# Expert loop of a two-layer trunk: down weights requested from ScalarE's queue instead of SyncE's

## The chip, the cores and the metric

The kernel runs on one core of one Trainium2 chip. The metric is the device time of one execution in microseconds. The engines are named as the profile names them: PE (TensorE), DVE (VectorE), ACT (ScalarE), POOL (GpSimd) and SP (SyncE). SP computes nothing here; it waits on semaphores and issues DMAs.

## What is computed

Two layers of a transformer trunk over 384 tokens of 1024 features (128 context tokens, 256 latent ones). Each layer has a mixing part (four attention-like branches) and then a mixture of experts. Only the latter is touched. Cut to what matters:

```python
scores = jax.nn.sigmoid((t @ lp['w_router']).astype(jnp.float32))
...
w = w / jnp.sum(w, axis=-1, keepdims=True) * ROUTE_SCALE
combine = jnp.sum(jax.nn.one_hot(eidx, N_EXPERTS, dtype=jnp.float32) * w[..., None], axis=1)
gu = jnp.einsum('nd,edf->nef', t, lp['w_exp_gu'])
a = jax.nn.silu(gu[..., :EXPERT_FF]) * gu[..., EXPERT_FF:]
a = (a * combine[..., None].astype(a.dtype)).reshape(-1, N_EXPERTS * EXPERT_FF)
routed = a @ lp['w_exp_down'].reshape(N_EXPERTS * EXPERT_FF, D_MODEL)
```

There are 32 experts a layer; every token goes to 4 of them. An expert has a gate-up matrix of 1024 x 512 (2 MB in fp32) and a down matrix of 256 x 1024 (1 MB).

## The kernel before

The tokens' choices are sorted into tiles of at most 96 rows, one expert a tile; an expert with more rows gets further tiles at the end. The loop over tiles goes two tiles a turn (`e` is 0 or 1, the tile's slot); the number of turns is read from a table, and here it is 16, so there are 32 tiles a layer and 64 in all.

For one tile the work is this. GpSimd gathers the tile's rows from DRAM into `xg` (`gather`, L1139). PE turns them (`turn_gathered`, L2337), ScalarE and VectorE split them into a rounded part and the rest (`x_high` L1454, `x_low` L1976). All products are made of three matmuls over such parts, so the weights are split as well: ScalarE rounds each landed gate-up half (`gu_high`, L1449) and VectorE writes the rest over it (`gu_low`, L1970); the same for the down weights (`dn_high`, L1461, two copies; `dn_low`, L1984). PE's `gate_up` (L2349) has 24 matmuls in two halves of 12, `down_split` (through L2051) 12. ScalarE takes the silu (L1492), VectorE the product (`product`, L1902), PE turns it (`turn_product`, L2293), ScalarE rounds that (L1485). The results of the down product stand in two banks of PSUM; ScalarE copies them to `yrow` (L1497, two copies a tile), and GpSimd scatters them to DRAM (`scatter`, L1150).

The order on each engine is written out in its own `steps(turn)`. PE's step for a tile is: turn the rows gathered for a later tile, turn the tile's product, gate-up of the next tile, down product of this tile. ScalarE's step is: round the gathered rows, round the turned product, round both gate-up halves for the tile after next, silu of the next tile, round the next tile's down weights, copy this tile's results. `W` holds two slots for gate-up weights (each two halves) and two for down weights.

All weights are asked for by SP (L943 for gate-up halves, L946 for down weights), one queue in the order of issue. Its step for a tile: once PE is through the first gate-up half of the next tile (`gu_half`), load that half for the tile after; once it is through the second, load the second; once this tile's down product has filled its second bank (`y1`), load the down weights of the tile after next into this tile's slot. The expert's number is read from a table in SBUF (`expert_u`, L973) ahead of each address. After the loop, in layer 0, SP loads the first four pieces of the next layer's weights (`load_front`, L993 and L997).

Of the kernel before, what the change touches and what calls it, by code (L numbers as in the profile page):

```python
# [19 lines left out]
P = 128  # L20
# [19 lines left out]
NE, TOPK, NG, TOPG, FF = 32, 4, 4, 2, 256  # L40
# [297 lines left out]
def trunk(nc, a):  # L338

    with ExitStack() as ctx:  # L340
# [3 lines left out]
        def sb_twice(name, n):  # L344
# [51 lines left out]
                 "gqa_ready", "kdup_ready", "diff_roped", "qm_roped", "km_ready", "max_ready",  # L396
                 "pd_ready", "lam_ready", "absx_ready", "expx_ready", "u_ready", "ln_ready", "lg_ready",
                 "dec_ready", "qkfb_ready", "masks_raw", "mask_ready", "state_ready", "state_out", "ro_ready",
                 "do_ready", "gate_ready", "merged_ready", "m_squared", "x_ready", "chosen_ready", "slots_ready", "ones_ready", "gathers", "sp_steps", "table_reset", "slots_out", "table_in", "rows_out", "tables_ready", "summed", "silu_ready",
                 "lam_dots", "lam_exps", "head_normed", "mean_ready", "ret_squared", "branch_rs"]  # L400
        names += ["bias_in0", "bias_in1", "bias_zero", "mod_gain", "gates_out", "gates_in", "cache_out"] + [f"{n}{i}" for n in ("x_landed", "y_written", "index_copied", "place_copied") for i in range(2)]
        names += [f"y_landed{i}" for i in range(3)]
# [3 lines left out]
        S = dict(zip(names + landed_names, sems))  # L406
# [109 lines left out]
        expert_f, expert_u = vm[:, 1124:1124 + NT], vm[:, 1172:1172 + NT].bitcast(U32)  # L516
# [65 lines left out]
        def expert_dn(s, tensor=W):  # L582
            return tensor[:, 2 * SLOT + s * SLOT // 2:2 * SLOT + (s + 1) * SLOT // 2].rearrange("p (k n) -> p k n", k=2)
# [42 lines left out]
        def job_filled(turn, e, name, less=0):  # L626
            return S["psum_filled"], in_turn(turn, e, name)[0] - less
# [46 lines left out]
        def keys_of(t):  # L674
            return (0,) if t == 0 else (1, 2, 3)
# [178 lines left out]
        for l in range(DEPTH):  # L854
# [3 lines left out]
            with nc.Block() as block:  # L858

                @block.sync  # L860
                def _(sp):
# [83 lines left out]
                    def load_down(s, src):  # L945
                        sp.dma_start(expert_dn(s), src.rearrange("(p k) n -> p k n", p=P)).then_inc(S[f"dn_landed{s}"], 16)  # L946

                    def expert(name, e):
                        return a[name].rearrange("l e d n -> (l e) d n")[bass.ds(e + l * NE, 1)].rearrange("o d n -> (o d) n")
# [21 lines left out]
                    def expert_of(tile):  # L971
                        sp.sem_inc(S["sp_steps"], 1)
                        return sp.value_load(expert_u[0:1, bass.ds(tile, 1)], min_val=0, max_val=NE - 1)  # L973

                    def steps(turn, last=False):
                        for e in range(2):
                            tile = turn * 2 + e
                            if not (last and e == 1):
                                sp.wait_ge(S["gu_half"], tile + 4)
                                src = expert("w_exp_gu", expert_of(tile + 3))  # L980
                                load_half(1 - e, 0, src)
                                sp.wait_ge(*job_filled(turn, e, "gu"))
                                load_half(1 - e, 1, src)
                            sp.wait_ge(*job_filled(turn, e, "y1"))
                            load_down(e, expert("w_exp_down", expert_of(tile + 2)))

                    with sp.Fori(0, turns - 2) as turn:
                        steps(turn)
# [12 lines left out]
                    for i in range(T * TOPK // 2):  # L1001
                        if i >= 3:
                            sp.wait_ge(S["summed"], 2 * (i - 2))
                        t, k = divmod(2 * i, TOPK)
# [172 lines left out]
                def _(act):  # L1177
# [128 lines left out]
                    for i in range(len(m) + 4):  # L1306
                        if i < len(m):
                            n = P * len(keys_of(m[i][2]))
# [60 lines left out]
                    for j in range(Z_PIECES, OUT_PIECES):  # L1369
                        kind, n, c, half = SPLITS[j]  # L1370
# [108 lines left out]
                    def steps(turn, last=False):  # L1479
                        for e in range(2):  # L1480
                            if not last:
                                act.wait_ge(*job_filled(turn, e, "xt1"))
                                x_high(e)
                            act.wait_ge(*job_filled(turn, e, "aT", LESS["turned"][e] if last else 0))
                            nc.scalar.activation(aT[:, e].rearrange("p f n -> p (f n)"), psum[:, BANK_AT, 0:2 * CAP],  # L1485
                                                 ACT.Copy).then_inc(S["a_high"], 1)
                            if not last:
                                gu_high(e, 0, turn * 16 + 32 + 16 * e)
                                gu_high(e, 1, turn * 16 + 32 + 16 * e)
                            if not (last and e == 1):  # L1490
                                act.wait_ge(*job_filled(turn, e, "gu", 2 if last else 0))
                                nc.scalar.activation(silu[0:CAP, 1 - e, :], psum[0:CAP, BANK_GU + 1 - e, 0:FF], ACT.Silu).then_inc(S["silu_ready"], 1)  # L1492
                                dn_high(1 - e, turn * 16 + 32)
                            act.wait_ge(S[f"y_written{e}"], turn * 16 + 16)
                            for c in range(2):
                                act.wait_ge(*job_filled(turn, e, f"y{c}", LESS["filled"][e] if last else 0))
                                nc.scalar.activation(yrow[0:CAP, e, c * C:(c + 1) * C], psum[0:CAP, BANK_Y + c, :], ACT.Copy).then_inc(S["act_emptied"], 1)  # L1497

                    with act.Fori(0, turns - 1) as turn:
                        steps(turn)  # L1500
# [934 lines left out]
```

## Time and profile before

| | |
|---|---|
| median of 3 runs | 2179.73 us (2178.5 to 2184.72) |
| the profiled execution | 2174.03 us, its span 2172.2 us |
| mean granted clock of PE in it | 0.939 |
| PE / DVE / ACT / POOL busy | 86% / 60% / 48% / 23% of the span |
| moved by SP's queue (q1), POOL's (q0), ACT's (q10) | 376.5 / 33.7 / 6.4 MB |

A page of the profile cuts the span in 40 equal slices and gives the busy share of each engine and of the DMA engines in tenths. Other views group the waits by who waited for whom, follow the chain of work that ended last, list the instructions in order of time, and give for each line how long its DMAs took from issue to landing. Times in them are microseconds from the span's start, durations of single instructions nanoseconds where that is said.

### The profile page before, as it was taken

How to read it: one execution, taken by the hardware profiler on the slowest of the kernel's cores; microseconds unless marked ns; L12 is line 12 of the kernel's file. 1: busy time of each engine (PE TensorE's matmuls, PEld its weight loads, DVE VectorE, ACT ScalarE, POOL GpSimd, SP SyncE). 2: the span in 40 equal slices, each digit the busy share in tenths (PEclk: the TensorE clock that was granted, in tenths of full speed). 3: DMA queues.
4: the chain of work that ended last, by engine and by line, in shares of the span. 5: the costliest groups of instructions: out<-in, count | busy, mean ns of one | idle time of the engine just before them, and what ended most of it. 6: DMA issues, size and time to landing. Idle time of an engine off the chain costs nothing. (4 is left out here: it accounts for less than half of the span.)

```text
span 2172.2 us, 27171 instructions
## 1 busy us (share of the span) xinstructions
PE 1867.6 (86%) x9234; PEld 1391.7 (64%) x9234; DVE 1300.6 (60%) x1857; ACT 1036.5 (48%) x1709; POOL 498.1 (23%) x430
## 2 busy tenths in 40 slices
PE   4999898999977699899649989989999767999992
PEld 2987566788864466666448866668887635666661
DVE  2244566634445578888753455665444475888885
ACT  2332247433332477777533423573333424877781
POOL 0002410400000445454100042114000022454540
PEclk8999899999998799999869999989999888999996
DMA  7543472233324399999834335403333336999994
GB/s 255 166 135 120 149 247 103 92 117 117 133 89 176 113 340 349 342 342 341 295 94 153 118 112 185 147 16 116 125 127 126 118 117 214 347 349 354 351 326 175
DMA packets 145062, 417.82 MB, mean 192 GB/s; under 512 B 26160, under 2 KB 36688, under 8 KB 118864
## 3 DMA queue, kind: packets, MB, share of 16 engines
q1 hardware_dynamic: 124208, 376.54, 50.0%
q0 software_dynamic: 17952, 33.74, 4.8%
q10 hardware_dynamic: 2816, 6.39, 0.8%
q8 instruction: 54, 0.88, 0.2%
q14 instruction: 32, 0.26, 0.0%
HBM read 409.70 MB, written 32.15 MB: 203 GB/s over the span
## 5 line engine op out<-in xcount | busy, mean ns | idle before, releaser
L1596 DVE TENSOR_TENSOR W_split<-W,W_split 128x2048 fp32r<-128x2048 f32 (+2 forms) x92 | 215.1, 2340 | 425.7 <-ACT W_split L1224 425.7
L2106 PE MATMUL psum<-W_split,qT_split 128*128 128x512 f32 (+3 forms) x1536 | 412.8, 381 | 15.9 <-PEq L2402 8.0
L1224 ACT ACTIVATE W_split<-W 128x2048 fp32r<-128x2048 f32 (+2 forms) x92 | 170.0, 1854 | 386.0 <-PE psum L2106 386.0
L2106 PEld LDWEIGHTS psum<-W_split,qT_split 128*128 128x128 f32 x1536 | 286.0, 191 | 71.4 <-issue 16.4
L2106 PE MATMUL psum<-W_split,scratch_split 128*128 128x512 f32 x864 | 280.5, 396 | 0.4 <-DVE hT_split L1591 0.4
L2106 PE MATMUL psum<-W_split,hT_split 128*128 128x512 f32 x576 | 213.7, 398 | 5.8 <-DVE scratch_split L1791 5.8
L2349 PE MATMUL psum<-W_split,zf_split 128*96 128x512 f32 x512 | 202.9, 396 | 0.0
L2106 PEld LDWEIGHTS psum<-W_split,scratch_split 128*128 128x128 f32 x864 | 162.2, 189 | 39.1 <-DVE hT_split L1591 0.6
L2106 PE MATMUL psum<-W_split,kT_split 128*128 128x512 f32 (+3 forms) x480 | 178.5, 372 | 0.0
L2106 PEld LDWEIGHTS psum<-W_split,hT_split 128*128 128x128 f32 x576 | 109.1, 190 | 31.6 <-DVE scratch_split L1791 6.3
L1146 POOL COPY vm<-vm 96x1 uint32 x64 | 64.4, 1006 | 242.7 <-ACT zf L1497 242.7
L1107 POOL DMA_DIRECT2D kT<-gate_rows x8 | 4.3, 547 | 503.2 <-PE psum L2058 356.0
L1139 POOL DMA_INDIRECT zf<-token_rows,vm x64 | 102.3, 1599 | 55.5 <-POOL vm L1136 55.5
L2349 PEld LDWEIGHTS psum<-W_split,zf_split 128*96 128x96 f32 x512 | 84.2, 164 | 32.0 <-issue 0.2
L2106 PEld LDWEIGHTS psum<-W_split,kT_split 128*128 128x128 f32 x480 | 92.1, 192 | 14.8
L2051 PE MATMUL psum<-W_split,zf_split 128*96 128x512 f32 x256 | 100.8, 394 | 0.0
L1970 DVE TENSOR_TENSOR W_split<-W,zf_split 128x2048 fp32r<-128x2048 f32 x32 | 73.3, 2291 | 35.1 <-ACT zf_split L1449 35.1
L1970 DVE TENSOR_TENSOR W_split<-W,qT_split 128x2048 fp32r<-128x2048 f32 x32 | 73.4, 2293 | 31.8 <-ACT qT_split L1449 31.8
L1267 ACT ACTIVATE Pb<-psum,nmax 128x384 f32<-128x384 f32 (+1 forms) x96 | 48.8, 509 | 88.5 <-DVE nmax L1668 87.6
L2349 PE MATMUL psum<-scratch_split,zf_split 128*96 128x512 f32 x256 | 89.0, 409 | 0.0
L2337 PE MATMUL psum<-const,zf 96*128 96x96 f32 x512 | 56.4, 256 | 36.6 <-DMA zf<-token_rows,vm 30.5
L2349 PE MATMUL psum<-qT_split,zf_split 128*96 128x512 f32 x256 | 85.5, 395 | 0.0
(341 smaller groups left out, 3940.2 us busy)
## 6 DMA issues: line engine op xcount, KB each, us to landing
W<-in_w_exp_gu SPq DMA_DIRECT2D x128, 1024.0 KB, 8.1
W<-in_w_exp_down SPq DMA_DIRECT2D x64, 1024.0 KB, 8.8
W<-in_w_in SPq DMA_DIRECT2D x60, 1024.0 KB, 5.1
W<-in_w_mod SPq DMA_DIRECT2D x40, 1024.0 KB, 5.3
W<-in_w_br SPq DMA_DIRECT2D x16, 1024.0 KB, 5.0
zf<-y_rows SPq DMA_DIRECT2D x12, 1024.0 KB, 6.9
W<-in_w_out SPq DMA_DIRECT2D x8, 1024.0 KB, 5.0
W<-in_w_mod SPq DMA_DIRECT2D x3, 2048.0 KB, 18.9
```

Source lines behind the costliest of these rows:

```text
L1107: pool.dma_start(gp[:, v, :], spread(a["gate_rows"][n, v])).then_inc(S["gates_in"], 16)
L1139: pool.indirect_dma_start(xg[0:CAP, e, :], None, a["token_rows"], bass.IndirectOffsetOnAxis(ap=index[0:CAP, e:e + 1], axis=0), bounds_chec ...
L1146: nc.gpsimd.tensor_copy(place_index[0:CAP, e:e + 1], entries[0:CAP, bass.ds(turn * 2 + e, 1), 1]).then_inc(S[f"place_copied{e}"], 1)
L1224: nc.scalar.activation(high(j), piece(SPLITS[j]), ACT.Copy).then_inc(S["high_ready"], 1)
L1267: nc.scalar.activation(Pb[:, (i % 3) * 384:(i % 3) * 384 + n], bank(("S",) + key, n), ACT.Exp, bias=nmax[:, i % 4:i % 4 + 1], scale=1.0, a ...
L1596: V.tensor_tensor(piece(SPLITS[j], Wr), piece(SPLITS[j]), high(j).bitcast(F32), ALU.subtract).then_inc(S["low_ready"], 1)
L1970: V.tensor_tensor(gu_half(e, h, Wr), gu_half(e, h), gu_wide(e, h).bitcast(F32), ALU.subtract).then_inc(S["gu_low"], 1)
L2051: ins = nc.tensor.matmul(dst, lhsT, rhs, start=(i == 0), stop=(i == len(pairs) - 1))
L2106: ins = nc.tensor.matmul(bank(job, piece_size(key)[1]), act_part[:, k0 + k, t * P:(t + 1) * P], w_part[:, k, :], start=first and (k, i) == ...
L2337: ins = nc.tensor.transpose(psum[:, BANK_XT + h, k * CAP:(k + 1) * CAP], xg[0:CAP, s, (4 * h + k) * P:(4 * h + k + 1) * P], ident[0:CAP, 0 ...
L2349: ins = nc.tensor.matmul(psum[0:CAP, BANK_GU + s, :], rows_x[:, 4 * h + k, :], cols_w[:, k, :], start=(h, k, i) == (0, 0, 0), stop=(h, k, ...
```

## The change

SP's step no longer waits for `y1` and no longer loads down weights. ScalarE's step, after its two copies of a tile's results, increments a semaphore of its own, reads the expert's number from the table, and issues the same load of the same bytes on its own queue. The loads ahead of the loop (the shared expert, experts 0 and 1) stay with SP, as do all gate-up halves. ScalarE issues none in the last turn, so the number of loads stays the same.

```diff
-                 ... "gathers", "sp_steps", "table_reset", ...
+                 ... "gathers", "sp_steps", "act_steps", "table_reset", ...
@@ SP, steps(turn, last)
                                 load_half(1 - e, 0, src)
                                 sp.wait_ge(*job_filled(turn, e, "gu"))
                                 load_half(1 - e, 1, src)
-                            sp.wait_ge(*job_filled(turn, e, "y1"))
-                            load_down(e, expert("w_exp_down", expert_of(tile + 2)))
@@ ScalarE, steps(turn, last)
                             for c in range(2):
                                 act.wait_ge(*job_filled(turn, e, f"y{c}", LESS["filled"][e] if last else 0))
                                 nc.scalar.activation(yrow[0:CAP, e, c * C:(c + 1) * C], psum[0:CAP, BANK_Y + c, :], ACT.Copy).then_inc(S["act_emptied"], 1)
+                            if not last:
+                                act.sem_inc(S["act_steps"], 1)
+                                used = act.value_load(expert_u[0:1, bass.ds(turn * 2 + e + 2, 1)], min_val=0, max_val=NE - 1)
+                                act.dma_start(expert_dn(e), a["w_exp_down"].rearrange("l e d n -> (l e) d n")[bass.ds(used + l * NE, 1)]
+                                              .rearrange("o d n -> (o d) n").rearrange("(p k) n -> p k n", p=P)).then_inc(S[f"dn_landed{e}"], 16)
```

## Rows read from the trace of the kernel before

**Rows 1.** The page: mean busy share of the DMA engines, 40 slices.

```profile
DMA  7543472233324399999834335403333336999994
```

**Rows 2.** Two stretches: length, busy us (count) of PE, PEld, DVE, ACT, POOL; PEclk, DMA share, GB/s.

```profile
1900.00:1950.00 50.00, 47.62 (x236) 33.95 (x235) 42.95 (x43) 40.25 (x51) 27.60 (x21) 1.00 0.98 350
...
24.00:26.00 2.00, 0.39 (x4) 0.30 (x3) 0.17 (x1) 0.00 (x0) 0.00 (x0) 1.00 1.04 387
```

**Rows 3.** Chain of waits, 1900 to 1924 us: start, us, what.

```profile
1903.54 8.58 DMA W<-in_w_exp_gu
...
1912.13 1.93 ACT zf_split L1449
...
1916.30 0.61 DVE zf L1902
...
1917.34 5.59 PE psum L2349 x24
...
1923.09 9.32 DMA W<-in_w_exp_gu
```

**Rows 4.** Chain: two gate-ups; line L946 between them; its landings (min/median/max).

```profile
1856.81 5.58 PE psum L2349 x24
...
2078.51 5.55 PE psum L2349 x24
...
L946 SPq DMA_DIRECT2D W<-in_w_exp_down x22: 337/338/338, 1866.0 to 2078.1; - x22
...
DMA to landing us min/median/max: 7.4/8.3/9.6
```

**Rows 5.** DMA issues at 1907.0 and at 1910.3 us: count, size, us to landing.

```profile
W<-in_w_exp_down SPq DMA_DIRECT2D x1, 1024.0 KB, 7.4
...
y_rows<-zf,vm POOLq DMA_INDIRECT x1, 5.0
```

**Rows 6.** Instructions of ACT and SP in order of time: start, us.

```profile
1904.76 1.06 ACT L1461 ACTIVATE qT_split<-W 128x1024 fp32r<-128x1024 f32 x1
1905.73 1.04 ACT L1461 ACTIVATE scratch_split<-W 128x1024 fp32r<-128x1024 f32 x1
1906.67 1.06 ACT L1497 ACTIVATE zf<-psum 96x512 f32<-96x512 f32 x2
1907.63 0.86 ACT L1454 ACTIVATE zf_split<-psum 128x384 fp32r<-128x384 f32 x2
...
1911.34 2.36 SPq L943 DMA_DIRECT2D W<-in_w_exp_gu  x2
```

**Rows 7.** Waits, 1850 to 2060 us: us in total, times, longest.

```profile
ACT zf_split L1449 <- DMA W<-in_w_exp_gu: 17.6, 10, 3.0
...
ACT qT_split L1449 <- DMA W<-in_w_exp_gu: 13.5, 10, 2.0
...
SPq L972 <- PE psum L2349: 61.4, 20, 4.0
```

**Rows 8.** ACT's queue by line (ns min/median/max); chain at 2096 and 2106 us.

```profile
L643 ACTq TENSOR_LOAD <-vm x2: 292/390/488, 744.6 to 1812.3; - x2
...
L1434 ACTq DMA_DIRECT2D token_rows<-zf x6: 387/530/743, 671.9 to 1737.8; - x6
...
2096.14 0.02 SPq L972
...
2096.93 9.75 DMA W<-in_w_exp_down
...
2106.70 0.04 ACT qT_split L1461
...
2106.78 0.04 ACTq L1496
```

**Rows 9.** The page's DMA issues (median landing); DMA queues, 1950 to 2000 us.

```profile
W<-in_w_br SPq DMA_DIRECT2D x16, 1024.0 KB, 5.0
...
q0 software_dynamic: 1135, 1.88, 11.9%
```

More of the change, by code:

```diff
@@ L398, in trunk @@
                  "dec_ready", "qkfb_ready", "masks_raw", "mask_ready", "state_ready", "state_out", "ro_ready",
-                 "do_ready", "gate_ready", "merged_ready", "m_squared", "x_ready", "chosen_ready", "slots_ready", "ones_ready", "gathers", "sp_steps", "table_reset", "slots_out", "table_in", "rows_out", "tables_ready", "summed", "silu_ready",
+                 "do_ready", "gate_ready", "merged_ready", "m_squared", "x_ready", "chosen_ready", "slots_ready", "ones_ready", "gathers", "sp_steps", "act_steps", "table_reset", "slots_out", "table_in", "rows_out", "tables_ready", "summed", "silu_ready",
                  "lam_dots", "lam_exps", "head_normed", "mean_ready", "ret_squared", "branch_rs"]
```

## The prediction

> **What bounds the kernel now.** First the page's DMA row [rows 1]. Of its 40 digits, each 54.3 us of the span, those from the 15th to the 19th and from the 35th to the 39th are nines: the two expert loops, one a layer. The change touches nothing else, so only these stretches are costed. In the second loop (first line of [rows 2]) the DMA engines are busy for a 0.98 share, 350 GB/s are moved, PE is busy 47.62 of 50 us and its granted clock is 1.00. The engines and the transfers are both nearly full, so the next question is which wait ends last.
>
> The chain of waits says it [rows 3]. A gate-up half is issued by SP at 1903.54 and lands 8.58 us later; ScalarE rounds it, VectorE takes the low part, multiplies out the waiting tile (0.61 us), PE turns that and runs its 24 gate-up matmuls (5.59 us), and their end lets SP issue the next half into that slot, at 1923.09. One round is 19.55 us for two tiles, and 8.58 of it is a landing. The rest, 10.97 us, is work. The round repeats: from the gate-up at 1856.81 to that at 2078.51 there are 22 tiles (as many down loads), so a tile takes 221.7 / 22 = 10.08 us [rows 4].
>
> Is the landing long because the chain is long, or because the transfers are full? 3 MB of weights a tile in 10.08 us are 312 GB/s; the rest of the 350 is GpSimd's gathers and scatters. While `w_mod` streams alone at the start, 387 GB/s are moved (second line of [rows 2]). An expert load takes about 8 us where a lone 1 MB load takes 5.0 [rows 4, 9]. In time of landing: a gate-up half at 1912.1 [rows 3], the down load behind it (issued 1907.0) 7.4 us after issue, at 1914.4 [rows 5], 2.3 us later. **The queue is never empty: the loop goes at the rate of its transfers**, and the waits of the engines only take up what is left. ScalarE waits 17.6 + 13.5 us for gate-up halves in 21 tiles, 1.5 us a tile [rows 7].
>
> **The change part by part.**
>
> *Bytes.* The same 30 loop loads of 1 MB a layer go, from another queue: 0 by themselves.
>
> *What SP loses.* A wait, a table read, a DMA issue. SP stands idle for PE's gate-up anyway (61.4 us in 210 on one line [rows 7]), and the wait it loses lies ahead of a later one on the same engine, PE. Worth 0: neither next half is issued sooner. Only at the end of layer 0 do two loads for the next layer (L993) go out earlier, now ahead of the last down load; it can be some 2 us later there. I put this at 0 to +2 us, once.
>
> *What ScalarE gains.* After the two copies of the results (L1497) a semaphore increment, the table read, some register work and a DMA issue. From rows of this trace: a table read on ScalarE's queue takes 0.29 to 0.49 us, a DMA issue there 0.39 to 0.74 [rows 8]; with SP's register work the sum is 0.9 to 1.5 us. SP itself needs 0.79 us from the end of its wait to the start of the issue [rows 8]. The trace has no table read of ScalarE in the loop. The low bound is 0.3: ScalarE's queue works on register instructions while a copy still runs (at 2106.78, under the rounding begun at 2106.70 [rows 8], which takes 1.06 us [rows 6]), so a 0.58 us copy can hide as much of 0.9. The high bound is 1.5. I take the middle, 0.9 us. The Trainium skill (DMA: Bandwidth & Descriptors, section "Latency and other measured facts") gives a floor of about 600 ns for such a read; the 0.29 to 0.49 measured here differ, and the measurement decides; with 600 ns the 0.9 would be, as an estimate, 1.1, and the sum below 11 us higher. Queued behind this on ScalarE are the rounding of the next gathered rows (L1454, 1907.63 [rows 6]), of the activations and of the next gate-up half. They run 0.9 us later. The cover is ScalarE's 1.5 us wait a tile for the second half [rows 7], so 0; where that wait shrinks, up to 0.9 us a tile is open.
>
> *When the down load starts.* SP issued at 1907.0 [rows 5]; ScalarE's second copy ends at 1906.67 + 1.06 = 1907.73 [rows 6], and with 0.9 the issue is near 1908.6, 1.6 us later.
>
> *The new cycle.* This is the term that decides. The down load issued in one tile is rounded by ScalarE (L1461) just ahead of the next tile's copies, behind which the next down load is now issued. So landing + rounding + copies + issue must fit into one tile. In the kernel before SP issued it on PE's word, and no such cycle of one tile existed. From the start of the rounding to the end of the copies are 1907.73 - 1904.76 = 2.97 us [rows 6]. The landing isn't in the trace, as the load always stood behind gate-up halves in one queue: low bound 5.0, a lone load [rows 9]; high bound 9.6, the longest in those 22 tiles [rows 4]. Queues do take turns: a scatter issued 3.3 us behind that down load (1910.3) landed in 5.0 us, at 1915.3, only 0.9 us after it [rows 5]. So the down load won't stand behind both halves; but it shares with GpSimd's indirect transfers (11.9% of the transfer time, 1.2 us of a tile [rows 9]) and with the next half, which SP issues 2.7 us after it (1911.34 [rows 6]); that half's first bytes cost it perhaps 0.2, an estimate. I take 5.0 + 1.2 + 0.2 = 6.4 us, nearer to the lone row, since the gate-up halves of that tile are nearly through when it starts (landed at 1912.1, 3.5 us after the new issue).
>
> *Sum.* 6.4 + 2.97 + 0.9 = 10.27 us a tile against 10.08: **+0.19 us**, on 28 steady tiles a layer, 56 in all: +10.6 us. With the one-time 0 to +2, +11 us. Against the profiled execution (span 2172.2, time 2174.0) that is 2185; the median of the runs shown is 5.7 us above that execution, and I predict for the median: 2179.7 + 11 = 2191. With the bounds of the issue alone (0.3, 1.5) the tile is 9.67 or 10.87: under 10.08 the transfers hold it and the gain is 0; above, +0.79 x 56 = +44 us at most, less in truth, since a longer tile thins the transfers and the landing nears 5.0 + 1.2.
>
> **Rivals.**
>
> *Nothing changes.* The rate of the transfers sets the tile, whoever asks for them; the new cycle fits in at 10.08 (a landing of 6.2 us or less). Time 2180, 5 us either way. For it: the share of 0.98, and that the landing adds up to 6.2 without the 0.2. Against it: it needs everything to fit to a few tenths of a us, and the spare transfers that now wait in SP's queue are gone. The Trainium skill (the same page, section "Issuing engines are not separate DMA queues") holds just this: the issuing engine saves only its own issue time. The 0.98 share agrees. Chance 0.28.
>
> *Faster: the gate-up halves get through sooner.* Now each half stands behind the down load before it. If two queues keep the DMA engines fuller, the rate rises from 350 toward the 387 seen at the start and the 8.58 us landing shrinks. PE then is the bound: it is idle 2.38 of 50 us [rows 2], 0.48 us of a tile, 27 us in all: 2153. It decides where more than 350 GB/s are to be had with two queues. For it: the 387. Against it: indirect transfers already make a second queue in the loop, and 0.98 is little room. Chance 0.15.
>
> *Much slower: the down load gets half the rate.* The gate-up halves are always in SP's queue, so the down load shares with them throughout, and each delays the other. With the 7.4 us landing of [rows 5] the tile is 11.27 us: +1.19 x 56 = +67, 2247. For it: landings of 7.4 to 9.6 now [rows 4]. Against it: a tile of 11.27 us leaves the DMA engines 10% idle, and then nothing is left to share with. Chance 0.12.
>
> **How the numbers follow.** The forecast has 0.45, with +3 to +28 us around its +11. A measurement of this kernel can tell about 0.3%, 6.5 us, from no change. Slower by more: 0.12 and 0.38 of the 0.45, with 0.01 of the first rival: 0.51. The same: 0.27 of the first rival, 0.06 of the forecast and 0.01 of the faster case: 0.34. Faster: 0.15. The range from 2160 to 2225 holds the forecast, the first rival and the better half of the faster one; outside lie some 0.07 below and 0.11 above.
>
> **What the profile after would show.** Right: down loads on ScalarE's queue landing in 6 to 7 us, a tile of 10.2 to 10.4, ScalarE's wait for the down load (L1461) up and that for the gate-up halves down, down loads on the chain of waits, the DMA share a little under 0.98. The first rival: a tile of 10.08 and the share unchanged, whatever lands when. The faster one: over 360 GB/s in the loop. The slow one: landings over 7.4 us on both queues. I am wrong at the root if the tile lengthens while ScalarE waits for neither load: then the issue itself is what costs.

## The result, and the profile after

The changed kernel takes 2196.8 us (median of 19 runs, 2188.3 to 2216.18), the kernel before, run beside it, 2180.3 (19 runs, 2169.07 to 2187.33): a ratio of **1.0083, 95% interval 1.0061 to 1.0105**. It is slower by 16.5 us. The profiled execution has a span of 2195.9 us against 2172.2.

The page of the changed kernel says first that the change did what it says: the down loads of the loop have moved from q1 to q10, byte for byte [rows 1 and the table before]. The DMA row still reads nine in nine of its ten loop slices and eight in the last: tenths are too coarse for this loss. The median landings of both kinds of load are even shorter than before (8.1 and 8.8 us there).

```profile
DMA  7544472233333499999734335303333327999984
...
q1 hardware_dynamic: 115568, 313.63, 41.3%
q10 hardware_dynamic: 11456, 69.31, 8.9%
...
W<-in_w_exp_gu SPq DMA_DIRECT2D x128, 1024.0 KB, 7.7
...
W<-in_w_exp_down ACTq DMA_DIRECT2D x60, 1024.0 KB, 8.0
```

Stretches of 50 us inside the loops show it more closely (columns as in [rows 2]). First the changed kernel:

```profile
850.00:900.00 50.00, 45.13 (x213) 32.06 (x214) 40.18 (x40) 36.72 (x47) 23.65 (x20) 0.97 0.93 324
...
2000.00:2050.00 50.00, 44.91 (x215) 31.68 (x213) 38.75 (x36) 36.21 (x46) 26.40 (x19) 0.97 0.95 329
```

and the same two stretches of the kernel before:

```profile
850.00:900.00 50.00, 46.73 (x232) 33.33 (x231) 42.73 (x41) 38.73 (x50) 28.39 (x20) 1.00 0.97 341
...
2000.00:2050.00 50.00, 47.03 (x233) 33.44 (x232) 42.87 (x42) 39.47 (x51) 27.27 (x20) 1.00 0.98 356
```

Over seven such stretches (four from 800 us, three from 1900) the DMA share is 0.96 to 0.99 before, 0.976 in the mean, and 0.93 to 0.97 after, 0.951 in the mean. The same bytes go through less busy DMA engines, not slower ones: for each unit of busy share they move 352 GB/s after and 355 before. So there are moments in which they have nothing to do. PE's granted clock is 1.00 in all seven stretches before and in two of seven after.

Two windows of 40 us, in slices of 1 us, show such a moment. First the kernel before, then the changed one, both from 2000 to 2040 us:

```profile
DMA  9898998999999999989989995998999999999799
```

```profile
DMA  8998998989988998989989999999998997737789
```

Worked out from the packets in the same way, for every slice from 800 to 1030 and from 1870 to 2080 us: of these 440 the engines are busy for under a half in 1 before and in 13 after.

The chain of waits gives the tile and what makes it longer [rows 3, 4]:

```profile
1862.48 7.10 PE psum L2352 x24
...
2013.29 11.07 DMA W<-in_w_exp_gu
...
2029.59 7.12 PE psum L2352 x24
...
2036.87 8.29 DMA W<-in_w_exp_gu
...
2112.93 5.08 PE psum L2352 x22
```

From the gate-up at 1862.48 to that at 2112.93 are 24 tiles (24 down loads are issued between), 10.44 us each against 10.08: +0.36 us. In the first loop the down loads of the changed kernel come every 10.57 us (21 of them from 809.5 to 1020.8), those of the kernel before every 10.29 (22 from 808.6 to 1024.7): +0.28. On 28 steady tiles a layer, the forecast's count, that is 10.1 + 7.7 = 17.8 us, about the 16.5 of the medians. The loss is in the steady loop.

One round shows where. The gate-up half issued at 2013.29 takes 11.07 us to land; the halves on the chain of the kernel before, from 1841 to 2074 us, take 8.58 to 10.51. Then the 24 matmuls take 7.12 us instead of 5.6. So the next half into that slot is asked for at 2036.87, 23.6 us after the last one, where the rounds of that chain before took 19.55 to 21.5. It is a bad round: others of the changed kernel are as short as before. The loads that land late are the **second gate-up halves**, which PE's gate-up waits for, not the down loads. From 800 to 1030 and 1870 to 2080 us they take 9.32 us in the mean before (43 loads) and 9.72 after (42), and their spread (standard deviation) grows from 0.88 to 1.24; first halves fall from 7.51 to 7.01 and down loads from 8.61 to 8.13. The other runs agree: with all loads on SP's queue the mean of the second halves is 9.42 (e1) and 9.34 (e5), with the down load split off 9.64 (e9) and 9.86 (e4). The waits of ScalarE say the same, in the window of [rows 7]:

```profile
ACT qT_split L1447 <- DMA W<-in_w_exp_gu: 21.1, 10, 3.9
...
ACT zf_split L1447 <- DMA W<-in_w_exp_gu: 18.9, 10, 3.4
...
ACT late_split L1459 <- DMA W<-in_w_exp_down: 2.1, 4, 1.2
...
ACT qT_split L1459 <- DMA W<-in_w_exp_down: 1.4, 1, 1.4
```

The waits for gate-up halves grew from 13.5 + 17.6 to 40.0 us, the longest from 3.0 to 3.9. Those for down weights fell to 3.5, from 11.4 in the kernel before:

```profile
ACT late_split L1461 <- DMA W<-in_w_exp_down: 7.6, 10, 1.7
...
ACT qT_split L1461 <- DMA W<-in_w_exp_down: 3.8, 7, 1.2
```

### The profile page after: what moved, and what is told of

Same layout as the page of the kernel before. It is cut to its first block and busy times, and to the rows that moved or that the text cites. A ratio compares the mean times of both kernels' runs of the same rounds, so it can differ in the third digit from the quotient of the medians.

```text
span 2195.9 us, 27144 instructions
## 1 busy us (share of the span) xinstructions
PE 1885.2 (86%) x9234; PEld 1400.6 (64%) x9234; DVE 1298.1 (59%) x1857; ACT 1037.1 (47%) x1710; POOL 501.9 (23%) x430
## 5 line engine op out<-in xcount | busy, mean ns | idle before, releaser
L2109 PEld LDWEIGHTS psum<-W_split,qT_split 128*128 128x128 f32 x1536 | 285.5, 190 | 72.2 <-issue 16.5
L2352 PE MATMUL psum<-W_split,zf_split 128*96 128x512 f32 x512 | 208.5, 407 | 0.0
L1144 POOL COPY vm<-vm 96x1 uint32 x64 | 78.6, 1228 | 259.3 <-ACT zf L1495 259.3
L2054 PE MATMUL psum<-W_split,zf_split 128*96 128x512 f32 x256 | 101.5, 396 | 0.0
L2352 PE MATMUL psum<-scratch_split,zf_split 128*96 128x512 f32 x256 | 94.2, 431 | 0.0
L1447 ACT ACTIVATE qT_split<-W 128x2048 fp32r<-128x2048 f32 x32 | 61.3, 1916 | 58.2 <-DMA W<-in_w_exp_gu 58.2
L2340 PE MATMUL psum<-const,zf 96*128 96x96 f32 x512 | 56.6, 256 | 36.7 <-DMA zf<-token_rows,vm 30.4
```

The source lines that it names most:

```text
L1144: nc.gpsimd.tensor_copy(place_index[0:CAP, e:e + 1], entries[0:CAP, bass.ds(turn * 2 + e, 1), 1]).then_inc(S[f"place_copied{e}"], 1)
L1447: nc.scalar.activation(gu_wide(e, h), gu_half(e, h), ACT.Copy).then_inc(S["gu_high"], 1)
L2054: ins = nc.tensor.matmul(dst, lhsT, rhs, start=(i == 0), stop=(i == len(pairs) - 1))
L2109: ins = nc.tensor.matmul(bank(job, piece_size(key)[1]), act_part[:, k0 + k, t * P:(t + 1) * P], w_part[:, k, :], start=first and (k, i) == ...
L2340: ins = nc.tensor.transpose(psum[:, BANK_XT + h, k * CAP:(k + 1) * CAP], xg[0:CAP, s, (4 * h + k) * P:(4 * h + k + 1) * P], ident[0:CAP, 0 ...
L2352: ins = nc.tensor.matmul(psum[0:CAP, BANK_GU + s, :], rows_x[:, 4 * h + k, :], cols_w[:, k, :], start=(h, k, i) == (0, 0, 0), stop=(h, k, ...
```

## The experiments

The landings gave the question. In the kernel before, all three loads of a tile stand in one queue and end one behind the other. Here are two loads of that kernel, in DMA views of a few tenths of a us: the second half issued at 2003.75 and the down load issued at 2007.29.

```profile
W<-in_w_exp_gu SPq DMA_DIRECT2D x1, 1024.0 KB, 10.0
...
W<-in_w_exp_down SPq DMA_DIRECT2D x1, 1024.0 KB, 9.3
```

They land at 2013.8 and 2016.6, 2.8 us apart. In the changed kernel, the second half issued at 2023.66 and the down load issued at 2027.36:

```profile
W<-in_w_exp_gu SPq DMA_DIRECT2D x1, 1024.0 KB, 11.9
...
W<-in_w_exp_down ACTq DMA_DIRECT2D x1, 1024.0 KB, 9.2
```

They land at 2035.6 and 2036.5, 0.9 us apart. Taking the landings of all expert loads in 800 to 1030 and 1870 to 2080 us, no two are closer than 2.2 us before (128 gaps), and 24 of 124 are under 2 us after. In both they land in the order in which they were asked for. But what has been moved by then differs. Between the issue of that down load and the landing of the second half ahead of it (the DMA view from 2027.4 to 2035.5 us), the queues of the changed kernel moved (packets, MB, share):

```profile
q10 hardware_dynamic: 142, 1.04, 37.9%
q1 hardware_dynamic: 130, 0.89, 32.1%
```

Nearly all of the down load's megabyte (q10) went through ahead of the end of the second half (q1), which was asked for 3.7 us sooner. Over both windows it is 0.80 of the megabyte in the mean of 42 pairs. And as the loads of a tile end together, little is left to move until PE's next gate-up lets SP ask again: the first half of the next tile is issued at 2035.60, just as the second half lands, and that is the digit 3 in the row of 2000 to 2040 us above.

From 800 to 1030 us the landings of gate-up halves (line L943, first and second together) are, in the kernel before and then in the changed one:

```profile
DMA to landing us min/median/max: 6.3/8.6/11.0
```

```profile
DMA to landing us min/median/max: 4.9/8.2/12.0
```

The median is shorter, and the longest longer: the loads come less evenly.

**Theories.** Either the two queues take turns, so that down bytes go ahead of the end of a second half that PE needs sooner; or ScalarE's added work is what costs; or the forecast's new cycle through the down load binds; or the lower granted clock of PE is a cause and not a mark; or issuing a load out of ScalarE's program, later and less evenly, is what costs, whichever queue it takes; or two queues as such make the transfers slower. The expectations below number them as they were put then; "theory 4" is the last of these in e7 and e8, and the one before it in e10.

### ScalarE's work alone: e1

```diff
+                            if not last:
+                                act.sem_inc(S["act_steps"], 1)
+                                act.value_load(expert_u[0:1, bass.ds(turn * 2 + e + 2, 1)], min_val=0, max_val=NE - 1)
```

The kernel before, with the increment and the table read behind the copies; SP goes on loading.

> The kernel before, with the semaphore increment and the table read of the change added behind ScalarE's copies, their value unused; SP still loads the down weights. Theory 1 (the down load on a queue of its own takes turns with the second gate-up half, which lands later; PE pauses, and its clock falls): the loads are as before, so the tile stays at 10.1 us, the clock in the loop at 1.00, the ratio to the kernel before within 0.3% of 1. Theory 2 (ScalarE's added work holds up its roundings): the part of it that the read makes shows, ratio 1.003 to 1.006. Theory 3 (the forecast: landing, rounding, copies and issue of the down load make a cycle of one tile): SP issues, no such cycle, ratio 1.

Measured: 2177.91 us, ratio 1.0004, interval 0.9988 to 1.0021. The increment and the read cost nothing that 12 runs can tell (0.2%).

### The down load made small, on either queue: e2 and e3

```diff
-   act.dma_start(expert_dn(e), ...)
+   act.dma_start(dn_eighth(e), ...[:, 1, 768:1024])
...
-   nc.scalar.activation(dn_wide(e, f), expert_dn(e)[:, f], ACT.Copy)
+   nc.scalar.activation(dn_wide(e, f).rearrange(...), dn_eighth(e)[:, None, :].to_broadcast([P, 4, 256]), ACT.Copy)
```

The loop's down loads bring 128 KB of the 1 MB, and ScalarE and VectorE read that eighth four times over for each half, so their work stays as it was; seven eighths of the weights are left out, and later routing may differ for it. e2 is the changed kernel so cut, e3 the kernel before (with the same edit at SP's load).

> The changed kernel with an eighth of each down load in the loop (128 KB; the rounding and the low part read this eighth repeated over the same widths, so the work on the engines keeps its size). To be read beside the kernel before with the same eighth, since results and so the second layer's routing differ from the kernel before. Theory 1: with 0.13 MB there is little to take turns with; the second gate-up half lands about as early as in its twin, and the first layer's loops differ by less than 0.1 us a tile. Theory 2: ScalarE's issue and read are all still there, so this stays slower than its twin by about 0.3 us a tile. Theory 3: the down load lands well under 5 us, no cycle binds, equal to its twin.

> The kernel before with an eighth of each down load in the loop, as in its twin. It also tests that the loop before goes at the rate of its transfers: 2.2 MB of weights a tile in place of 3. If that holds, the tile falls from 10.1 us to where PE is the bound, 9.2 to 9.6 us, the first layer's loop by 15 to 25 us, and DMA's share to under 0.85. If the chain of engines were the bound and the transfers only nearly full, the tile stays within 0.2 us of 10.1.

Measured: e2 2146.28 us, ratio 0.9855 (0.9827 to 0.9884); e3 2147.94 us, 0.9856 (0.9834 to 0.9878). With little in the load, the two kernels differ by nothing that four runs of each can tell (0.3%). In the first loop the tile takes 9.73 us (e2) and 9.69 (e3), a little over the 9.2 to 9.6 expected. Here the transfers have room, so a small cost of ScalarE's issue or of the second queue could be hidden; what is shown is that the loss needs a big load or full transfers. With the DMA share down to 0.78 (e2) and 0.83 (e3) from 1900 to 1950 us, both gain 1.4%: the loop did go at the rate of its transfers.

### The clock: e4 and e5

In the round shown above PE stands idle for 2.30 us ahead of 2029.20, and then runs at the lower of its two levels: a granted clock of 0.50, 1.2 GHz, in the stretch below. That is why the 24 matmuls took 7.12 us. In the whole execution 13 of the 64 gate-ups take over 5.9 us, in the kernel before 4, and the time above 5.58 adds up to 21 us against 5. By size alone this could be the whole loss, so it had to be tried.

```profile
2030.50:2033.80 3.30, 3.30 (x10) 2.12 (x9) 3.30 (x5) 1.70 (x1) 2.41 (x3) 0.50 0.94 312
```

```diff
                                 turn_gathered(e)
+                                for _ in range(2):
+                                    nc.tensor.matmul(psum[0:CAP, 7, 0:256], const[:, 0:CAP], const[:, 128:384], start=True, stop=True)
```

Two matmuls of constants a tile, whose result nobody reads, keep PE busier. e4 adds them to the changed kernel, e5 to the kernel before.

> The changed kernel with two more matmuls a tile on PE, 96 x 256 of constants into the eighth bank that the loop does not use, behind the turning of the gathered rows, where PE then waits for VectorE's product. If the fall of the clock (0.97 in the loop's stretches after, 1.00 before) is a part of the loss, and not just a mark of the pauses, the clock stays at 1.00 and some 10 of the 17 us come back: ratio to the kernel before 1.002 to 1.005. If the clock costs nothing, as the time lost in slow matmuls is had back from the next wait for a landing: 1.008 or more, up to 1.015 by the matmuls added.

> The kernel before with the same two matmuls of constants a tile that were put into the changed kernel: the price of these matmuls where the clock never falls. The changed kernel with them came out at 1.0114, its clock fell 3 times in the loops in place of 10. If this control comes out at 1.006 or more, the steadier clock did give back what it seemed to cost (0.3 to 0.5%), and the matmuls took it again. If it stays within 0.3% of 1, the matmuls are nearly free and the clock's fall was not what cost the time; it only marked the pauses.

Measured: e5 2179.45 us, 1.0000 (0.998 to 1.002); e4 2200.97 us, 1.0114 (1.0088 to 1.014). The matmuls are free in the kernel before, and they do bring the clock back in the changed one: 5 gate-ups over 5.9 us where that has 13, and 14 in its second trace (e9); a clock of 1.00 in five of the seven stretches, against two and, in e9, four; a mean granted clock over all runs of 0.936 (median of 6), as in the kernel before (0.935), where the changed kernel has 0.931. The time does not come back, and the DMA share falls all the same:

```profile
1900.00:1950.00 50.00, 47.61 (x234) 33.85 (x233) 41.98 (x40) 37.53 (x48) 25.31 (x20) 1.00 0.92 330
```

In e4's first loop a tile still takes 10.62 us. The lower clock is a mark of PE's pauses and not the cause of the loss.

### The forecast's cycle, made to bind: e6

```diff
                                 gu_high(e, 0, turn * 16 + 32 + 16 * e)
+                            if not (last and e == 1):
+                                ask_down(turn, e)
+                            if not last:
                                 gu_high(e, 1, turn * 16 + 32 + 16 * e)
```

The changed kernel with the increment, read and issue moved behind the rounding of a first gate-up half of the next tile (`ask_down` is the same four lines, for the tile before). It was meant to come some 1.5 us later. In the trace the issue stands 4.1 us behind the end of the down product in the median of 39 loads (1.8 to 8.6), where the changed kernel has 0.88 (42 loads): 3.3 us later, of which a part may be the cycle's own doing.

> The changed kernel with ScalarE's down load issued some 1.5 us later, behind the rounding of the next tile's first gate-up half (that is where the forecast put it). Theory 1 (turns with the second gate-up half): less of the down load runs beside that half, which lands earlier than the 9.6 to 9.8 us of the changed kernel; if nothing else binds, the ratio falls to 1.000 to 1.005. Theory 3 (the cycle of landing and rounding of the down load): it has only 5.7 us until ScalarE wants it, so ScalarE's wait for it grows from 4 us in 210 to 20 or more, and the ratio rises to 1.010 to 1.030. If both are at work, the wait grows and the halves land earlier at once.

Measured: 2225.21 us, 1.0201 (1.0174 to 1.0228). Here the chain runs through the down loads, one after the other, and ScalarE waits for them between 1870 and 2080 us:

```profile
1911.13 8.50 DMA W<-in_w_exp_down
...
1924.00 10.43 DMA W<-in_w_exp_down
```

```profile
ACT late_split L1458 <- DMA W<-in_w_exp_down: 19.0, 8, 6.8
ACT qT_split L1458 <- DMA W<-in_w_exp_down: 17.7, 8, 6.0
...
ACT zf_split L1446 <- DMA W<-in_w_exp_gu: 11.3, 7, 2.8
...
ACT qT_split L1446 <- DMA W<-in_w_exp_gu: 6.2, 6, 1.9
```

36.7 us for down weights and 17.5 for gate-up halves; the changed kernel has 4.4 and 40.4 there. The forecast's cycle exists, and binds when the issue is that much later. In the changed kernel it doesn't bind.

### Other loads on the second queue: e7, e8, and the changed kernel again: e9

```diff
@@ e7: SP, steps
-                                sp.wait_ge(*job_filled(turn, e, "gu"))
-                                load_half(1 - e, 1, src)
@@ e7: ScalarE, behind the silu; e8 takes the first half in the same way, between its two gu_high
+                                    used = act.value_load(expert_u[0:1, bass.ds(turn * 2 + e + 3, 1)], min_val=0, max_val=NE - 1)
+                                    act.dma_start(gu_half(1 - e, 1), ...[:, 4:8, :]).then_inc(S[f"gu_landed{1 - e}1"], 16)
```

e7 is the kernel before with the second gate-up half on ScalarE's queue; first half and down weights stay with SP. In e8 it is the first half that moves, so that the second half and the down load keep their order in one queue.

> The kernel before with the second gate-up half (the one on the chain of waits) issued by ScalarE's queue, once PE is through the one before, and first half and down load left with SP. Theory 1: now the half on the chain is the one that need not stand behind the others; it lands in 7 to 8.5 us from its issue in place of 9.1 to 9.6, and the ratio is 0.995 to 1.002 (the transfers still set the rate). Theory 4 (two hardware queues as such lower the rate of the transfers): under 345 GB/s in the loop and 1.005 to 1.010, as in the changed kernel, whichever load goes alone. If the issue comes much later than SP's, behind ScalarE's other work, that delay shows on the chain and adds to either.

> The kernel before with the first gate-up half, which is not on the chain of waits, issued by ScalarE's queue (just ahead of the rounding of a second half, once PE is through the half before); second half and down load stay on SP's queue in that order. Theory 1 (the loss comes from the down load no longer standing behind the second half): the order is kept, the second half lands as in the kernel before or earlier (9.0 to 9.6 us, none over 11), the tile is steady, ratio 0.997 to 1.003. Theory 4 (two hardware queues as such make the transfers slower or unsteady): ratio 1.005 to 1.010, stretches under 330 GB/s as in the changed kernel and in the one with the second half alone.

> The changed kernel as it is, on the same chip and beside the same runs of the kernel before as the one above: 1.006 to 1.010 as measured first. Its trace is a second sample of how late the second gate-up halves land and in how many places the clock falls; Theory 1 asks for longest landings of the gate-up halves of 11.5 us or more again, against 10.3 to 11.0 in the kernel before.

Measured: e7 2195.84 us, 1.0078 (1.0055 to 1.0101); e8 2187.74 us, 1.0034 (1.0013 to 1.0054); e9 2200.82 us, 1.0102 (1.007 to 1.0133), the changed kernel's loss again, with longest landings of 11.6 and 12.3 us as theory 1 asked. Every split loses. For e7 theory 1 had said 0.995 to 1.002 and a second half that lands in 7 to 8.5 us; it lands in 8.95 in the median, so being alone in a queue doesn't put a load ahead. e8, which keeps the second half ahead of the down load, loses least, and lies between the numbers of its two theories. Its second halves land sooner (8.7 us in the median, none over 10.9) and no stretch moves under 335 GB/s; there ScalarE now waits for the first halves, the load that is alone in its queue (800 to 1030 us; in the kernel before these two waits are 1.0 and 0.8 us there):

```profile
ACT hT_split L1448 <- DMA W<-in_w_exp_gu: 13.9, 7, 3.9
ACT scratch_split L1448 <- DMA W<-in_w_exp_gu: 8.5, 8, 3.0
```

These runs left two readings: the order in which bytes are served, or issuing from ScalarE, which in e7 issued the half 0.89 us after the gate-up's end, in the median, where SP takes 0.17. (e7, e8 and e10 also peel one turn off ScalarE's loop and have GpSimd write its first rows of `y_spare` in two parts.)

### All three loads from ScalarE, in one queue: e10

```diff
@@ SP: its steps in the loop are taken out
@@ ScalarE: first half as in e8, second half as in e7, down load as in the changed kernel
```

> The kernel before with all three weight loads of a tile issued by ScalarE: the first half behind its rounding of a first half, as in e8, the second behind the silu, as in e7, the down load behind the copies, as in the changed kernel. So the three go through one queue again, in the old order (first half, second half, down), but all are issued by ScalarE and at the moments of the split versions; SyncE issues none of them. Theory 1 (the loss comes from two queues taking turns, which makes the gate-up halves late and uneven): ratio 0.997 to 1.003; landings of the second half 9.0 to 9.7 us with a maximum under 11.2; three landings of a tile 2 us or more apart; at most two falls of the granted clock in the steady loops. Theory 4 (the loss comes from issuing out of ScalarE's program, later or less evenly than SyncE does, whichever queue it is): ratio 1.008 or more, at least as much as the changed kernel, with ScalarE's issues 0.5 us or more behind SyncE's. Between 1.003 and 1.008 both have a share.

Measured: 2181.71 us, **1.0008 (0.9989 to 1.0027)**. The loads are issued by ScalarE, the down load and the second half from the same places as in the changed kernel and e7 (0.88 us after the end of the down product and of the gate-up, in the median), and the loss is gone. The page shows that they share one queue, and their landings:

```profile
q10 hardware_dynamic: 28160, 190.95, 24.7%
...
W<-in_w_exp_gu ACTq DMA_DIRECT2D x116, 1024.0 KB, 8.2
...
W<-in_w_exp_down ACTq DMA_DIRECT2D x60, 1024.0 KB, 8.4
```

The DMA engines are as full as in the kernel before (1 of the 440 slices is busy for under a half), and ScalarE's waits for down weights, 1870 to 2080 us, are back at 13.2 us, as they were under one queue:

```profile
1900.00:1950.00 50.00, 46.58 (x229) 33.00 (x228) 42.52 (x41) 39.35 (x51) 25.85 (x20) 1.00 0.99 347
```

```profile
ACT late_split L1447 <- DMA W<-in_w_exp_down: 7.7, 9, 2.0
...
ACT qT_split L1447 <- DMA W<-in_w_exp_down: 5.5, 9, 1.3
```

Of the landings that can be paired with their issues (105 gaps) none is under 2.2 us. Two of the expected signs missed: the second halves land in 8.9 and 8.6 us in the median of the two windows (22 of 43 can be paired), under the 9.0 named, being issued later, and the granted clock is under 1.00 in three of the seven stretches where two falls were allowed. Issuing from ScalarE is not what costs. Splitting the loads over two queues is. Nor are two queues slower as such: for each unit of busy share e10 moves 351 GB/s, the changed kernel 352.

### The same order by hand, in one queue: e11 and e12

```diff
@@ e11: SP, steps; load_half(.., 1, ..) and load_down now load in pieces, 768 + 256 KB and 512 + 512 KB
-                                load_half(1 - e, 1, src)
+                                load_half(1 - e, 1, src, ((0, 3),))
                             sp.wait_ge(*job_filled(turn, e, "y1"))
-                            load_down(e, expert("w_exp_down", expert_of(tile + 2)))
+                            down = expert("w_exp_down", expert_of(tile + 2))
+                            load_down(e, down, (0,))
+                            if not (last and e == 1):
+                                load_half(1 - e, 1, src, ((3, 4),))
+                            load_down(e, down, (1,))
```

What does a second queue do? If all it does is to let down bytes ahead of the last bytes of the second half, then one queue with that order must lose too. e12 is the control: the same pieces, in the old order.

> The kernel before, all loads from SyncE's one queue, with the second gate-up half cut into a piece of 768 KB and one of 256 KB and the down load into two of 512 KB. They are issued in the order: first half, 768 KB of the second half, then behind the wait for the down product's second bank: first 512 KB of the down weights, the last 256 KB of the second half, last 512 KB of the down weights. So a single queue here is given by hand an order in which a part of the down load stands ahead of the end of the second half, as two queues that take turns would give it. Theory A (order is the mechanism: the second half ends later because down bytes go ahead of its last bytes): second half's last piece lands about 1.5 us later after its tile's first issue than in the control e12 (512 KB at the loop's 350 GB/s), ratio at least 1.005 above the control's, likely 1.01 to 1.02. Theory B (two queues cost by themselves, by how the engines alternate between them): within 0.003 of the control.

> Control of e11: the same four pieces, in the old order (first half, 768 KB and 256 KB of the second half, then behind the wait both 512 KB pieces of the down weights). Both theories: 0.997 to 1.003 against the kernel before; more than 1.003 if smaller pieces and SyncE's two added issues cost something themselves, and e11 is then read against this run.

Measured: e12 2184.88 us, 1.0028 (1.001 to 1.0046); e11 2221.18 us, **1.0193 (1.0158 to 1.0228)**, 1.0165 times its control. SP's issues in e11 (in order of time: start, us, line; L947 is a piece of the second half, L951 one of the down weights), and the chain's landing of the last piece:

```profile
2007.79 0.33 SPq L947 DMA_DIRECT2D W<-in_w_exp_gu  x1
2011.20 0.34 SPq L951 DMA_DIRECT2D W<-in_w_exp_down  x1
2011.73 0.33 SPq L947 DMA_DIRECT2D W<-in_w_exp_gu  x1
2012.25 0.33 SPq L951 DMA_DIRECT2D W<-in_w_exp_down  x1
```

```profile
2011.73 7.14 DMA W<-in_w_exp_gu
```

The control's, for the second half begun at 2017.17:

```profile
2017.68 9.44 DMA W<-in_w_exp_gu
```

In e11 the half is whole at 2018.87, 11.1 us after its first piece was issued (2007.79), in e12 at 2027.12, 9.95 us after. That is 1.1 us, a little under the 1.5 expected; over both windows it is 10.57 us (39 halves) against 9.72 (42), 0.85 us, and it costs 1.6% of the time. The last piece is also asked for later in e11, 4.0 us after the first in place of 0.5; but three loads asked for before it were then still to land (at 2012.53, 2015.27 and 2017.45), so it was its place in the queue that it waited for. The stretches look like those of the changed kernel, only more so: first e11, then e12.

```profile
1950.00:2000.00 50.00, 41.76 (x197) 29.52 (x195) 35.14 (x33) 35.16 (x44) 20.11 (x16) 0.93 0.88 307
```

```profile
1950.00:2000.00 50.00, 46.17 (x227) 32.77 (x226) 41.31 (x39) 39.21 (x50) 22.16 (x20) 1.00 0.98 336
```

In one queue, issued by the engine that always did, a second half that ends later loses time, empties the DMA engines (under a half busy in 24 of the 440 slices, in the control in 1) and lowers the clock. The order of the bytes is enough to cause each of the signs that the changed kernel shows. The price is much the same too: 1.65% for 0.85 us here, 0.83% for 0.40 us there. Whether it is the whole of the 0.8% isn't settled: e8 kept that order for the second half and the down load and still lost 0.3%. There it is the first half that shares its time with the two others and comes late; e10 issues it from the same place, in one queue, without that loss.

## Why the prediction was right, and for which wrong reason

The direction was right, and so was the size in the rough: 2191 forecast, 2196.8 measured, inside 2160 to 2225 (+11 us forecast, +16.5 measured); the tile came to 10.44 us, just over "10.2 to 10.4". The mechanism was not the one named, so that the number fell near is luck: the +0.19 us a tile was what a cycle would have run over the tile, and that cycle doesn't bind. Of the signs named for "right" only the longer tile and the lower DMA share came; the down loads' landing, both waits of ScalarE and the down loads on the chain did not come.

- **The loop goes at the rate of its transfers:** right. An eighth of the down bytes gave 1.4% in either kernel (e2, e3).
- **Bytes, and what SP loses, 0:** no run speaks against either as a cost of its own; e10 takes all of SP's loop away and costs nothing. But moving the bytes to another queue, the 0 of "Bytes", is what cost. The one-time 0 to +2 us at the end of layer 0 wasn't tried alone.
- **ScalarE's added work hidden:** right (e1, 1.0004). With e10 even three such steps a tile are hidden.
- **"When the down load starts", 1.6 us later:** wrong. The step put the issue behind the end of the copies. The rows show otherwise:

```profile
1987.03 0.36 ACTq L1499 DMA_DIRECT2D W<-in_w_exp_down  x1
...
2026.47 1.04 ACT L1459 ACTIVATE qT_split<-W 128x1024 fp32r<-128x1024 f32 x1
2027.36 0.35 ACTq L1499 DMA_DIRECT2D W<-in_w_exp_down  x1
2027.42 1.05 ACT L1459 ACTIVATE scratch_split<-W 128x1024 fp32r<-128x1024 f32 x1
2028.37 1.07 ACT L1495 ACTIVATE zf<-psum 96x512 f32<-96x512 f32 x2
```

  These are ScalarE's instructions in order of time. At 2027.36 the load goes out ahead of the copies that precede it in the program, and even ahead of the second rounding (L1459). ScalarE's queue doesn't wait for the copies to run. So what sets the issue is the end of the down product, as for SP: one ends at 1986.12 and the load follows at 1987.03, 0.91 us later. In the kernel before one ends at 2037.01 and SP issues at 2037.83, 0.82 us later. Over both windows the medians are 0.88 us (42 loads, 0.87 to 3.0) and 0.82 (43, 0.80 to 0.93): the load goes out 0.06 us later, not 1.6. The forecast had seen this working ahead at 2106.78 [rows 8] and used it only for a low bound.
- **"The new cycle", the term that decided:** wrong. It held landing 6.4 + 2.97 + 0.9 = 10.27. Without the wait behind the copies the cycle is slack: ScalarE's wait for down weights fell from 11.4 to 3.5 us, where the forecast had it rise, and no down load stands on the chain between 1846 and 2127 us. e6, in which the issue is 3.3 us later, has that cycle: waits of 36.7 us and +2.0%. What the forecast's 1.6 us would have cost was not run. The landing of 6.4 us in that sum was too low as well: 8.1 in the mean of 42 down loads.
- **"That half's first bytes cost it perhaps 0.2":** this is the sentence that held the true mechanism, with only one side of it. The loads do share; the down load lands in 8.0 us in the median, not in 6 to 7. But what the kernel pays is the other direction: what the down load takes from the second gate-up half, 0.40 us in the mean, which the sum put at nothing. That half isn't a new wait; it is the old one of [rows 3], made longer and uneven. PE then pauses, SP asks for the next half later, the DMA engines run dry for a moment (13 slices against 1), and where the transfers set the rate this is not made up.
- **Wrong at the root, if the tile lengthens while ScalarE waits for neither load:** not so, it waits more for gate-up halves (31.1 to 40.0 us, [rows 7]).

The rivals. *Nothing changes* was next in chance. Its rule, from the Trainium skill (DMA: Bandwidth & Descriptors, section "Issuing engines are not separate DMA queues"), holds that asking from several engines saves only issue time. No time is saved here, but the measurement differs in that the split costs 0.8%, and that e10, with one queue on ScalarE, costs nothing. *Faster* fell: no stretch moves more than before, 324 to 347 GB/s against 341 to 356. *Much slower* had the sign that came true (landings over 7.4 us on both queues: 8.0 and 7.7) and the half of the mechanism that counts, "each delays the other". It put the price on the down load's own cycle, 11.27 us a tile; that cycle doesn't bind.

The Trainium skill (DMA: Bandwidth & Descriptors, section "Queues, rings and completion order") says that a DMA engine goes round between the queues that have work for it, packet by packet. The trace agrees: 0.80 of the down load's megabyte went ahead of the end of a second half asked for before it, and landings came 0.9 us apart in two queues and never under 2.2 in one.

## What to carry to other kernels

In this loop, which its transfers bound, one queue was a schedule: loads landed in the order in which they were asked for, 2.2 us or more apart, and the load that the critical chain waits for could be put ahead. Moving another big load to a second queue gave that up. They still landed in the order of their issue, but most of the later one went ahead of the end of the earlier one; here that cost 0.8% though the load was asked for only 0.06 us later, and no split of the three loads was faster than one queue. When a forecast moves an issue to another engine, ask first what stood behind or ahead of it in its old queue, and which of those loads the chain waits for.

## What the runs showed of the hardware that was not expected

- ScalarE's queue issues a DMA ahead of compute instructions that stand before it in the program: at 2027.36, 1.0 us before the copies at 2028.37 begin. In e10 it issued three megabyte loads a tile without loss (1.0008).
- Two queues moved no more than one, 335 GB/s in the mean of seven stretches against 347, with the 16 engines at 0.95 against 0.98. Every run with full megabyte loads in two queues, or with bytes mixed by hand (e11), has 10 or more slices of 1 us in 440 with the engines busy for under a half; the kernel before, e1, e5, e10 and e12 have 0 to 2.
- Two matmuls a tile bring the slow gate-ups from 13 down to 5 of 64 and don't bring back a microsecond (e4, 1.0114 against 1.0083 and 1.0102).
- Smaller pieces in the same order cost a little: 1.0028 (1.001 to 1.0046) for 256 to 768 KB in place of 1 MB, with a DMA share of 0.98 to 1.00 (e12).
